# GpSimd's scatters paced by ScalarE's counts instead of TensorE's, in a hybrid attention and expert-retrieval block on one core

## The reference, cut to what matters

```
s_top, i_top = lax.top_k(scores, 16)                 # per half of the query, of 128 keys
best, pos = lax.top_k(s_top[0][:, None] + s_top[1][None, :], 16)
gates = softmax(best)                                # 8 heads x 16 picks = 128 experts per token
act = gelu(einsum('td,tkd->tk', h, expert_u[idx]))
out = einsum('tk,tkd->td', act * gates, expert_v[idx])
x <- LayerNorm(alpha * x + out)
```

## Time and profile before

| what | value |
|---|---|
| runs | 1816.7, 1817.13 and 1829.67 us; median 1817.13 us |
| the profiled execution: its time, its span | 1816.11 us, 1814.4 us |
| its mean granted TensorE clock | 0.993 of full speed |
| TensorE busy | 1782.6 us (98%) |
| VectorE, ScalarE, GpSimd busy | 1257.8, 739.1 and 1033.9 us |

### The profile page before, as it was taken

The page is one execution under the profiler, slowest core; times in us unless marked ns, Lnnn a source line. Parts: engine busy times, 40 slices in busy tenths (PEclk is TensorE's granted clock), DMA queues, the critical chain, the costliest instruction groups (busy, mean ns, idle before and its releaser), DMA issues.

```text
span 1814.4 us, 25731 instructions
## 1 busy us (share of the span) xinstructions
PE 1782.6 (98%) x9402; PEld 1511.6 (83%) x9402; DVE 1257.8 (69%) x2436; ACT 739.1 (41%) x1225; POOL 1033.9 (57%) x771
## 2 busy tenths in 40 slices
PE   9999999999999999999989999999999999999998
PEld 6777778887888888888889999998888888888886
DVE  6334261112588999898857777773599989988886
ACT  5734463222243323333445655553443333333331
POOL 6432414343253467787776677665588887777410
PEclk9999999999999999999989999999999999999999
DMA  5764643235132344444434544446899999999971
GB/s 195 253 211 147 185 129 98 88 104 186 59 105 82 117 151 136 149 143 147 130 111 141 162 154 160 150 140 208 317 374 382 392 390 388 391 372 371 370 271 70
DMA packets 189967, 368.69 MB, mean 203 GB/s; under 512 B 27905, under 2 KB 109953, under 8 KB 189714
## 3 DMA queue, kind: packets, MB, share of 16 engines
q1 hardware_dynamic: 101216, 209.74, 34.3%
q10 hardware_dynamic: 53810, 89.90, 13.9%
q0 software_dynamic: 34816, 67.41, 10.1%
HBM read 305.96 MB, written 61.01 MB: 202 GB/s over the span
## 4 chain that ended last, share of the span: by engine, by line
PE 93%; DMA 2%; ACT 2%; DVE 1%; issue 1%; another core or an unknown queue 1%; POOL 0%; ACTq 0%; SPq 0%; DVEq 0%
PE bank L578 24%; PE bank L582 24%; PE bank L581 24%; PE bank L958 18%; DMA x<-in_x 1%; PE bank L870 1%; PE bank L741 1%; PE bank L714 1%; PE bank L727 1%; PE bank L787 0%; DMA gates<-gate_scratch 0%; DMA xT_raw<-in_xT 0%; PE bank L796 0%; DMA stage<-in_mix_stream 0%
## 5 line engine op out<-in xcount | busy, mean ns | idle before, releaser
L536 POOL DMA_INDIRECT gate_scratch<-scat_gate,scat_idx x384 | 445.8, 1161 | 180.8 <-issue 97.0
L486 POOL TENSOR_TENSOR w_lo<-stage,w_hi 128x1024 fp32r<-128x1024 f32 (+1 forms) x105 | 248.5, 2387 | 374.7 <-ACT w_hi L1044 338.5
L1044 ACT ACTIVATE w_hi<-stage 128x1024 fp32r<-128x1024 f32 (+1 forms) x284 | 292.4, 1042 | 175.8 <-PE bank L582 148.7
L578 PE MATMUL bank<-x_hi,w_lo 128*128 128x512 f32 (+1 forms) x864 | 336.6, 390 | 0.8 <-issue 0.6
L582 PE MATMUL bank<-x_hi,w_hi 128*128 128x512 f32 (+1 forms) x864 | 334.5, 387 | 0.0
L581 PE MATMUL bank<-x_lo,w_hi 128*128 128x512 f32 (+1 forms) x864 | 334.5, 387 | 0.0
L578 PE MATMUL bank<-w_hi,wt_lo 128*128 128x512 f32 x768 | 298.9, 389 | 0.4 <-DVE wt_lo L1936 0.4
L582 PE MATMUL bank<-w_hi,wt_hi 128*128 128x512 f32 x768 | 298.8, 389 | 0.0
L581 PE MATMUL bank<-w_lo,wt_hi 128*128 128x512 f32 x768 | 298.8, 389 | 0.0
L1677 DVE TENSOR_TENSOR w_lo<-stage,w_hi 128x1024 fp32r<-128x1024 f32 x178 | 216.9, 1221 | 72.0 <-ACT w_hi L1044 49.5
L523 POOL DMA_INDIRECT gat<-in_expert_v,eidx x128 | 154.0, 1203 | 112.1 <-DVE bank L1661 63.5
(11 more groups left out here) (289 smaller groups left out, 3130.8 us busy)
## 6 DMA issues: line engine op xcount, KB each, us to landing
stage<-in_expert_uT SPq DMA_DIRECT2D x128, 512.0 KB
stage<-in_expert_v SPq DMA_DIRECT2D x128, 512.0 KB
stage<-in_mix_stream SPq DMA_DIRECT2D x84, 512.0 KB
gate_scratch<-zeros SPq DMA_DIRECT2D x32, 768.0 KB, 7.4
act<-activation_scratch ACTq DMA_DIRECT2D x32, 768.0 KB
gates<-gate_scratch ACTq DMA_DIRECT2D x32, 768.0 KB
activation_scratch<-act_out_a ACTq DMA_DIRECT2D x64, 256.0 KB
activation_scratch<-act_out_b ACTq DMA_DIRECT2D x64, 256.0 KB
```

The costliest lines, as they stand in the source:

```text
L486: nc.gpsimd.tensor_tensor(w_lo[:, slot, 0:width], stage[:, slot % STAGE, 0:width], w_hi[:, slot, 0:width], ALU.subtract).then_inc(split_do ...
L536: nc.gpsimd.indirect_dma_start(out=gate_cells, out_offset=bass.IndirectOffsetOnAxis(ap=scat_idx[:, b, k:k + 1], axis=0), in_=scat_gate[:, ...
L578: ins = mm(dst, l_lo, r_hi, start=first, stop=False)
L1044: act_f(w_hi[:, slot, 0:width], stage[:, slot % STAGE, 0:width], ACT.Copy).then_inc(hi_done, 1)
```

## The change

Three waits of GpSimd get other semaphores. The scatters of the pair stage wait for ScalarE's count of rounded weight parts, 7 further on than the product they waited for and at most 224; the scatters before and behind it wait for the same number of gelus as they waited for tiles; and the first gather waits for the 128th gelu instead of TensorE's last score tile. Nothing else differs: the order of the scatters, all increments and every other wait stay.

```
+def part_due(cell):
+
+    return min(product_due(cell) + 7, 7 * PAIRS)
...
                 if EARLY_CELLS <= cell < EARLY_CELLS + PAIR_CELLS:
-                    pool.wait_ge(prod_done, product_due(cell))
+                    pool.wait_ge(part_hi, part_due(cell))
                 elif tile_due(cell) > tile_due(cell - 1):
-                    pool.wait_ge(quarter_used, first_expert + tile_due(cell))
+                    pool.wait_ge(gelu_done, tile_due(cell))
                 scatter(cell)
 
             pool.wait_ge(eidx_ready, 1)
-            pool.wait_ge(quarter_used, first_value)
+            pool.wait_ge(gelu_done, NKEY)
             for k in range(4):
                 gather_row(k)
```

## The result

The change makes the kernel slower: median 1838.62 us (5 runs, 1834.73 to 1853.92) against 1816.7 us (5 runs), a ratio of 1.0141 with the 95% interval 1.0112 to 1.0169. The profiled execution took 1853.92 us; it is the slowest of the five, so its rows show more loss than the median has. I had forecast 1817 us and no difference, range 1803 to 1830.

A forecast was written before the change was run, and what follows sets the result against it. The prediction took TensorE to bound the kernel, busy 1782.6 of 1814.4 us. Its terms were all 0: 1816.1 + 0 + 0 + 0 = 1816.1 us for the profiled execution, so a median of 1817 us, range 1803 to 1830.

The forecast's parts named there:

- The sum's first term: Pair stage, scatters 155 to 370 waiting for rounded parts: cost 0, bounds -20.0 to +13.8 us.
- Rival A: Expert stages: TensorE's unexplained time hangs on GpSimd's waiting for its products; faster, 1802 or 1796 us; chance 0.14.
- GpSimd is mainly limited by itself: Pair stage, 905 to 1240 us: scatters and issue fill 278.4 of 335 us; only 52.5 us of waits can move.
- Theory T: Formed after the result: TensorE falls behind during GpSimd's back-to-back indirect DMAs, catches up in pauses; product waits time those pauses.
- Rival B: A further slow stretch of TensorE from shifted work, clock and DMAs; slower, 1830 us; chance 0.12.
- Rival C: From cell 155 on, GpSimd falls behind and the table's load is late; slower, 1839 us; chance 0.06.
- the port: SBUF port pair shared by VectorE and GpSimd: scatters rise 0.1 us each, 21 us, inside existing waits; priced at 0.
- The late scatters and the first gather: Pair stage's end: cell 371 about 2.3 us later, first gather at most 0.6; cost 0, bounds +1.0 and +0.6 us.

The follow-up runs named there:

- pair_only: Kernel before with only the waits of scatters 155 to 370 changed, from product to rounded part; ratio 1.0131.
- no_pair_scatters: Changed kernel with scatters 155 to 370 left out, so their gates are missing; 1798.5 us, ratio 0.9895.
- the two landing kernels: Kernel before with a landing wait at every sixth pair-stage scatter, product waits 9 later at the start or unchanged; ratios 1.0432 and 1.0421.
- gelu_only: Kernel before with only the waits on tiles and the first gather moved to gelus; ratio 1.0045.
- landing_every_6: Changed kernel, pair-stage scatters free-running but for a wait at every sixth for earlier scatters to land; ratio 1.0221.
- products_in_14s: Kernel before with its waits on TensorE's products rounded down to every 14th; ratio 1.0007.
- calm group: Two of five run groups: kernel before at 1786.2 and 1785.4 us, profiled kernels without unexplained TensorE waits from 800 us on.
- parts_plus_10: Changed kernel with its wait 3 parts later, still on ScalarE's count; ratio 0.9997 in a calm group, 1.0143 in another.
- products_minus_7: Kernel before with each wait on TensorE's products 7 products earlier; ratio 1.0002 in a calm group, 1.0039 in another.
- part_and_product: Changed kernel with the old wait for TensorE's product added behind the new one for ScalarE's part; ratio 1.0002.

## Why the prediction was wrong

*The sum's first term.* It failed at "I take 0, since the row nearest to it, TensorE's waits, names no scatter". An unexplained wait names nobody, so it can't acquit GpSimd. Measured: `pair_only` +1.3%, 23.5 us. My upper bound for this term, "one more stretch like that of 900:930, +13.8 us", was too low as well: the median moved by 21.9 us, and with no pacing wait the term is 260 us. My measure of a stretch was itself a little high, since it counts the waits and the clock's share over each other: in 900:930 TensorE did 148 matmuls of the 252 that it does undisturbed, which is 12.4 us lost and not 13.8.

*Rival A, with its sign turned.* I had the link between GpSimd and TensorE's unexplained time as a rival, but tied it to GpSimd's waiting. Against it I put that "GpSimd waited for nothing but its own issue, and TensorE was slow all the same". That row was the evidence for what the runs show: GpSimd's issuing can hold TensorE up, and without the scatters the stretch is gone. I read the 2.61 us of wait at the end of the stretch as a consequence and didn't ask why TensorE recovered in just that pause. The possible gain was real (`no_pair_scatters`, -1.0%), but it lay in fewer scatters.

*"GpSimd is mainly limited by itself".* Right as a reading, and the 52.5 us of waits were rightly called all that can be moved. Their total hardly changed (55.1 us). But they had a function that I didn't see: by Theory T, a scatter that waits for TensorE's product keeps GpSimd quiet while TensorE is behind.

*Rival B* foretold a further slow stretch, as chance. There was one in the value stage, worth 10.1 us of idle time and 3% of the clock over 200 us, and those of the pair stage grew; without scatters the pair stage has none, so chance was the wrong reason. *Rival C* wasn't what happened, but its price, one for one behind the load of the table, showed in the two landing kernels. Its cause, the port, was no part of it: scatters took 1.12 us at most in the mean. Nor do the two scatters of 0.96 and 1.39 us make a rule: the one at 904.52 took 0.96 us too, beside a VectorE part that ran from 904.53 to 905.25.

*The late scatters and the first gather.* Right in their size. Cell 371 started 0.3 us behind the gelu that ends at 1266.57, the first gather 0.8 us behind the gelu of tile 127, and TensorE's first value matmul still waits 0.38 us for VectorE alone:

```profile
1266.84 0.95 POOL L541 DMA_INDIRECT gate_scratch<-scat_gate,scat_idx  x1 [11.20 <-ACT act_out_b L1378]
...
1305.73 0.97 POOL L528 DMA_INDIRECT gat<-in_expert_v,eidx  x1 [22.63 <-ACT act_out_b L1302]
```

```profile
1304.63 0.47 PE L583 MATMUL bank<-w_hi,wt_lo 128*128 128x512 f32 x1 [0.38 <-DVE wt_lo L1941]
```

VectorE's wait for the first gathered weights grew from 4.43 us to 6.48. Against the start of the value stage they come 0.9 us later, and of the slack of 1.6 us some 0.7 was left. What wasn't foreseen is the +0.45% of `gelu_only`, with three of ten executions some 20 us above the others; its profiled one lost 11.6 us between 1285 and 1400, most of it while gathers were issued without a pause. Why these executions and not the others stays open.

**What is shown and what isn't.** Shown: where before takes some 1817 us, scatters issued by GpSimd without pause in the pair stage bring TensorE to a near standstill, memsets in their place don't, and pacing by ScalarE's count costs 1.2 to 1.4% against TensorE's. Argued only: that ScalarE's count harms because it comes in bursts and stands a cycle ahead. It fits that the kernels which lose 1.2 to 1.4% have 42 to 51 such waits, `landing_every_6` with 2.2% has 31, and those within 0.5% of before have 59 to 66; `products_in_14s` was to test it and fell in a calm group. Open: by which path TensorE is held up, why the scatters ahead of the pair stage cost nothing, why the slowness can outlast them, and why two of the five groups don't show it. There four kernels with other waits for the scatters (`parts_plus_10`, `products_minus_7`, `products_in_14s`, `part_and_product`) agree with before within 0.1%. The changed kernel itself wasn't run there; by its neighbour `parts_plus_10` it would cost nothing. No kernel here beats the one before with its output whole.

## What to carry to other kernels

Unexplained ("issue") waits of the busiest engine have a place in time: lay them beside what every other engine issues, and look at what changes in the moment when they end, before calling an edit of an idle engine free. Look also at a stretch where the same thing is issued and nothing is lost: it tells that the explanation is not complete. A wait can be a governor: here the waits of GpSimd's indirect DMAs on TensorE's products were worth 1.2 to 1.4%, though nobody waited for their data. Where two kernels are compared, run the reference kernel beside them each time, since the kernel before itself took 1.6% more in one group of runs than in another on the same chip, and in the faster group no pacing of the scatters made a difference.

## What the runs showed of the hardware

- GpSimd's indirect DMAs (128 elements of 4 bytes, one in 1.27 us) slowed TensorE from 836 to 35 matmuls of 128x256 in 100 us, with the DMA engines 2% busy, and TensorE did 7 matmuls in the 15 us behind the last of them. Ahead of the pair stage, beside matmuls of mostly 128x512, 42 of them in 68 us cost nothing. TensorE also lost time beside gathers in the value stage, in some executions.
- The same stream did nothing to TensorE in two groups of five: 1086 matmuls in 130 us beside 93 scatters, and 1786 us where the others have 1815 to 1822 for the same kernel.
- Plain DMAs of the same shape took GpSimd about half the time to issue (541 ns against 974), but a packet took 95 ns against 12, the DMA engines were at 0.84 for 46 GB/s, and VectorE waited up to 26.9 us for a store to land.
